# Where the first four weight slots behind a norm are split: all in front of it, or one in front and three among the scaled chunks

## What is computed

```python
def rms_norm(x, g):
    y = x * rsqrt(mean(x * x, -1) + 1e-5)
    return y * g
h = x
p = rms_norm(h, norm_mix) @ w_in                        # "mix"
...
h = h + square(relu(rms_norm(h, norm_mlp) @ w_up)) @ w_down     # "mlp"
x = rms_norm(h, norm_final)                             # "final"
n = rmsnorm(x, g0) * (1 + scale0) + shift0              # "g0", scale and shift from silu(c) @ ada_w
z = gelu(n @ a_w_in) ...                                # its v half is the stage "a_v"
x = x + gate0 * mixed
n = rmsnorm(x, g1) * (1 + scale1) + shift1              # "g1"
x = x + gate1 * conv_ffn(n)                             # "ffn"
```

## Time and profile before

| | us |
|---|---|
| median of three runs | 2870.2 (2868.9 to 2871.1) |
| the profiled execution, its own time | 2871.4 |
| its span in the trace | 2869.5 |
| PE busy | 2745.0 (96%) |
| DVE busy | 2027.0 (71%) |
| ACT busy | 1399.7 (49%) |
| POOL busy | 177.8 (6%) |

### The profile page before, as it was taken

How to read it: one execution, slowest core, us unless ns; L and a number is a source line. 1 busy time by engine, 2 the same in 40 slices (tenths; PEclk the granted TensorE clock), 3 DMA queues, 4 the chain that set the end, 5 groups by cost and what they waited for, 6 DMA issues and landing times.

```text
span 2869.5 us, 48840 instructions
## 1 busy us (share of the span) xinstructions
PE 2745.0 (96%) x17766; PEld 2358.8 (82%) x17766; DVE 2027.0 (71%) x3149; ACT 1399.7 (49%) x2217; POOL 177.8 (6%) x210
## 2 busy tenths in 40 slices
PE   7999988799799999999999999999989999999997
PEld 6878877688588888888886888888868888888886
DVE  5676555577688787888888776668877756665675
ACT  5444443455554444444454455445455545554553
POOL 4600000030100000000020000000100000000002
PEclk9999999899899999999999999999999999999999
DMA  5554200245367778777776874567745555555553
GB/s 192 181 164 163 97 2 2 100 166 188 128 246 281 273 279 292 272 278 279 272 274 222 295 264 164 180 232 276 277 148 184 187 189 181 193 184 188 187 179 137
DMA packets 157857, 573.42 MB, mean 200 GB/s; under 512 B 18000, under 2 KB 18416, under 8 KB 157264
## 3 DMA queue, kind: packets, MB, share of 16 engines
q1 hardware_dynamic: 154368, 562.11, 56.6%
q10 hardware_dynamic: 2208, 7.57, 0.7%
q0 software_dynamic: 1072, 0.89, 0.1%
HBM read 567.64 MB, written 2.10 MB: 199 GB/s over the span
## 4 chain that ended last, share of the span: by engine, by line
PE 83%; DVE 9%; POOL 3%; issue 2%; ACT 2%; DMA 0%; ACTq 0%; DVEq 0%; POOLq 0%
PE ps L2212 44%; PE ps L2213 24%; PE ps L2215 3%; DVE wlo L1896 3%; PE ps L2237 2%; PE ps L2239 2%; PE ps L2238 2%; PE ps L1002 1%; ACT whi L1681 1%; DVE tt L1923 1%; DVE tt L1981 1%; PE ps L1001 1%; PE ps L990 1%; PE ps L1572 0%; POOL tab L285 0%
## 5 line engine op out<-in xcount | busy, mean ns | idle before, releaser
L1896 DVE TENSOR_TENSOR wlo<-raw,whi 128x1024 fp32r<-128x1024 f32 x872 | 1060.9, 1231 | 429.4 <-ACT whi L1681 427.7
L2212 PE MATMUL ps<-xn,whi 128*128 128x512 f32 x3540 | 1259.3, 400 | 11.5 <-issue 5.3
L1681 ACT ACTIVATE whi<-raw 128x1024 fp32r<-128x1024 f32 x872 | 905.0, 1054 | 593.9 <-PE ps L2213 515.0
L2213 PE MATMUL ps<-xn,wlo 128*128 128x256 f32 x3776 | 1052.5, 281 | 0.0
L2212 PE MATMUL ps<-act_in,whi 128*128 128x512 f32 x2444 | 868.5, 400 | 7.7 <-issue 3.4
L2212 PEld LDWEIGHTS ps<-xn,whi 128*128 128x128 f32 x3540 | 667.8, 189 | 177.4 <-issue 11.1
L2213 PE MATMUL ps<-act_in,wlo 128*128 128x256 f32 x2624 | 730.6, 281 | 0.0
L2213 PEld LDWEIGHTS ps<-xn,wlo 128*128 128x128 f32 x3776 | 716.0, 190 | 5.1
L2212 PEld LDWEIGHTS ps<-act_in,whi 128*128 128x128 f32 x2444 | 461.2, 189 | 121.2 <-DVE wlo L1896 5.0
L2213 PEld LDWEIGHTS ps<-act_in,wlo 128*128 128x128 f32 x2624 | 497.6, 190 | 4.0
L1688 ACT ACTIVATE hl<-ps 128x256 f32<-128x256 f32 x416 | 155.3, 375 | 356.9 <-PE ps L2215 356.9
(11 more groups left out here) (329 smaller groups left out, 2226.0 us busy)
## 6 DMA issues: line engine op xcount, KB each, us to landing
raw<-in_stream SPq DMA_DIRECT2D x872, 512.0 KB, 4.2
adaw<-in_ada SPq DMA_DIRECT2D x96, 512.0 KB, 5.9
adaq<-in_ada SPq DMA_DIRECT2D x96, 512.0 KB, 4.8
h<-in_xT SPq DMA_DIRECT2D x4, 512.0 KB, 7.4
memx<-in_memT ACTq DMA_DIRECT2D x1, 2048.0 KB, 9.3
out<-fin SPq DMA_DIRECT2D x4, 512.0 KB, 2.6
lwa<-in_lora ACTq DMA_DIRECT2D x1, 1536.0 KB, 6.9
wst<-in_wsT ACTq DMA_DIRECT2D x1, 1024.0 KB, 8.4
```

What stands on the lines that cost most here:

```text
L1681: act.activation(whi[:, r, :], raw[:, r, :], ACT.Copy).then_inc(hi_done, 1)
L1896: dve.tensor_tensor(wlo[:, r, :], raw[:, r, :], whi[:, r, :].bitcast(F32), ALU.subtract)\
L2212: pe.matmul(ps[:, b, :], whi[:, r, w], x[:, kc, :], start=first, stop=False)
L2213: ins = pe.matmul(ps[:, b, 0:T], wlo[:, r, w], x[:, kc, 0:T], start=False, stop=False)
```

## The change

Behind the norms `mlp`, `g0` and `g1` the split of the next stage's first four slots is taken out of the stage before (`LATE`). Slot 0 is split by ACT in front of the norm and by DVE behind its small steps; slots 1 to 3 are split among the chunks of `prepare`: on DVE after chunks 2, 4 and 6; on ACT slot 1 in front of chunk 0 and slots 2 and 3 in front of chunks 3 and 5. The same at the kernel's beginning, where also: `ones` is set by POOL and not loaded; ACT loads the table of the root ahead of the squares (it holds the square too) and does `silu` after `prepare`; PE does 20 matmuls of `ones` with `ones` (128 x 128) before its first sum and waits for `ident` only before the spread.

```diff
+    LATE = ("q", "o", "mlp", "a_uo")
...
+        pool.memset(ones[:, :], 1.0).then_inc(cols_zero, 1)
...
-        act.dma_start(ones[:, :], A["const"][:, C_ONES, :]).then_inc(const_in, 16)
...
             for j in chunks:
+                if ahead and j in (3, 5):
+                    ahead(0, (j + 1) // 2)
                 act.wait_ge(xp_done, XP[nm] + j + 1)
...
-                     nm == "w_in" or nm in AHEAD.values(), split(L[AHEAD[nm]]) if nm in AHEAD and nm != "q" else None, aside, nm in TAIL_FIRST)
+                     nm == "w_in" or nm in AHEAD.values(), split(L[AHEAD[nm]]) if nm in AHEAD and nm not in LATE else None, aside, nm in TAIL_FIRST)
...
         act.wait_ge(cols_zero, 2)
+        preload(act, ACT.Sqrt)
         for q in range(4):
             act.wait_ge(x_in[q], 16)
             squares(h, tt, 0, range(4 * q, 4 * q + 4))
-        for p in range(RING):
-            split(L["w_in"])(0, p)
+        split(L["w_in"])(0, 0)
+        norm("mix")
+        split(L["w_in"])(0, 1)
+        prepare("mix", ahead=split(L["w_in"]))
         act.wait_ge(par_in, 16)
-        act.wait_ge(cols_zero, 2)
         act.activation(silu_c[:, :], col("c", 0, DC), ACT.Silu).then_inc(silu_done, 1)
-        norm("mix")
-        prepare("mix")
...
+        split(L["mlp"])(0, 0)
         norm("mlp")
-        prepare("mlp")
+        split(L["mlp"])(0, 1)
+        prepare("mlp", ahead=split(L["mlp"]))
...
                 if j:
                     low(j - 1)
+                if ahead and j in (2, 4, 6):
+                    ahead(0, j // 2)
...
-        for p in range(RING):
-            split(L["w_in"])(0, p)
         norm("mix", EPS_1)
-        prepare("mix", h, lambda j: col("norm_mix", j))
+        split(L["w_in"])(0, 0)
+        prepare("mix", h, lambda j: col("norm_mix", j), ahead=split(L["w_in"]))
...
         norm("final", EPS_1)
         norm("g0", EPS_2)
+        split(L["a_v"])(0, 0)
...
-        prepare("g0", h, lambda j: nfg[:, j:j + 1], 0)
+        prepare("g0", h, lambda j: nfg[:, j:j + 1], 0, ahead=split(L["a_v"]))
...
-        pe.wait_ge(const_in, 32)
-        pe.wait_ge(cols_zero, 5)
+        pe.wait_ge(cols_zero, 6)
+        for _ in range(20):
+            pe.matmul(ps[:, stat_bank["mix"] + 2, 0:P], ones[:, :], ones[:, :], start=True, stop=True)
...
+        pe.wait_ge(const_in, 16)
         spread("mix")
```

More of the change, by code:

```diff
@@ L1699, in norm, with prepare @@
             act.activation(y, x, ACT.Sqrt, scale=-2.0).then_inc(rs_done, 1)
-        def prepare(nm, shift=None, chunks=range(DC)):
+        def prepare(nm, shift=None, chunks=range(DC), ahead=None):
             dst, x = act_in if nm == "cross" else xn, sqm if nm == "mem" else tt
             for j in chunks:
+                if ahead and j in (3, 5):
+                    ahead(0, (j + 1) // 2)
                 act.wait_ge(xp_done, XP[nm] + j + 1)
@@ L1816, in _ @@
         rows("g0", ada, 16)
+        split(L["a_v"])(0, 1)
         act.wait_ge(mod_done, 1)
@@ L1819, in _ @@
         act.dma_start(bsb[:, :, :], A["bsb"]).then_inc(mix_in, 16)
-        prepare("g0", 0)
+        prepare("g0", 0, ahead=split(L["a_v"]))
         def a_v(lin, i, g, b):
@@ L1847, in _ @@
         run("a_uo", a_uo)
+        split(L["ffn"])(0, 0)
         norm("g1")
         rows("g1", adb, 8)
-        prepare("g1", 48)
+        split(L["ffn"])(0, 1)
+        prepare("g1", 48, ahead=split(L["ffn"]))
         def ffn(nm, up):
@@ L1961, in scale_of, with prepare @@
             return ps[:, spread_bank[nm], 0:T]
-        def prepare(nm, src, gain, shift=None, chunks=range(DC)):
+        def prepare(nm, src, gain, shift=None, chunks=range(DC), ahead=None):
             dst, x = act_in if nm == "cross" else xn, sqm if nm == "mem" else tt
@@ L2067, in _ @@
         norm("mlp", EPS_1)
-        prepare("mlp", h, lambda j: col("norm_mlp", j))
+        split(L["mlp"])(0, 0)
+        prepare("mlp", h, lambda j: col("norm_mlp", j), ahead=split(L["mlp"]))
         def mlp(lin, i, g, t):
@@ L2137, in _ @@
         norm("g1", EPS_2)
+        split(L["ffn"])(0, 0)
         dve.wait_ge(ada_red, 4)
         modulation(64, 32, 64, "g1")
-        prepare("g1", h, lambda j: mod[:, 96 + DC + j:97 + DC + j], 48)
+        prepare("g1", h, lambda j: mod[:, 96 + DC + j:97 + DC + j], 48, ahead=split(L["ffn"]))
         dve.memset(zc[:, :, 0:1], 0.0).then_inc(pads, 1)
```

## The result

The changed kernel is slightly slower, 0.1 to 0.3%; the interval of the ratio leaves out 1.

What follows compares the result with a forecast made beforehand. PE, busy 96% of the span, was taken as the bound. Terms -4.8 (beginning with tables), +0.1 (`mlp`), +3.4 (`g0`), +0.1 (`g1`) and 3 x 1.5 (clock) gave +3.3 on 2870.2: 2873.5 us, range 2866.5 to 2879.

Steps and rivals of the forecast that it cites:

- sums end: At the beginning, after the warm-up, eight chunks at full clock and eight slow: sums end near 18.7, not 23.84.
- beginning at slot 4: First chunk of `w_in` 8.4 us earlier, but splits and `silu` delay slot 4: ready at 41.5, not 45.02; -3.5 us.
- clock behind it: Low clock after PE's new wait for slot 4: +1.5 us each at the beginning, `mlp` and `ffn`, bounds 0 and 2.5.
- wait for the tables gone: POOL starts the tables earlier, so PE's 1.26 us wait behind ACT's 4.37 us wait for them goes: -1.3 us.
- `mlp` at slot 4: First chunk 3.3 us earlier, slot 4 3.4 later behind it: +0.1 us before the clock.
- `a_v` at slot 4: At `g0` the first chunk stays and three splits lengthen PE's wait: +3.4 us, bounds 2.8 and 4.2.
- Rival E: Faster: the ring does not gate slot 4, head starts stay and no clock falls, about 2856 us; chance 0.05.
- Rival C: At the beginning the warm-up's clock holds through all sums, first chunk at 18.3, total 2870.3 us; chance 0.12.
- rival D: Slower: PE's clock is lost for longer, the warm-up gives nothing, slot 4 at 46.4; 2878.4 us; chance 0.15.
- `silu`: At the beginning ACT's `silu` with its table load, ahead of slot 4's split, delays that split by 1.5 us.
- A: The forecast itself, clock falls charged at the beginning, `mlp` and `ffn`: 2873.5 us, spread 2871 to 2876.5; chance 0.45.
- B: PE's waits grow as forecast but the clock falls at one site or none: about 2869.5 us; chance 0.20.

Runs made afterwards that it cites:

- `a_v` alone: Only the splits of `a_v` moved behind the norm, the beginning, `mlp` and `ffn` as in the kernel before: 2880.8 us, ratio 1.0017 to before.
- two inside: Changed kernel with two splits among the chunks in place of three, `silu` later, root's table earlier, `a_v` as before: 2863.8 us, ratio 0.9966 to before.
- three in front: Changed kernel with three of `a_v`'s splits ahead of the modulation at `g0` and one among the chunks: 2874.2 us, ratio 1.0014 to before.
- without `a_v`: Changed kernel with the norm `g0` and the stage `a_v` put back as before: 2871.7 us, ratio 0.9991 to before.
- again: The kernel before, unedited, profiled a second time: 2872.5 us.
- `mlp` and `ffn` alone: Only the norms `mlp` and `g1` changed, the beginning and `a_v` as in the kernel before: 2874.5 us, ratio 1.0000 to before.
- beginning alone: Only the beginning changed, the three later norms as in the kernel before: 2870.2 us, ratio 0.9983 to before.
- `silu` later: Changed kernel with ACT's `silu` moved from in front of slot 4's split into the groups of `w_in`: 2873.3 us, ratio 1.0003 to before.

## Why the prediction came out as it did

| term | forecast | trace of after |
|---|---|---|
| sums end | 18.7 | 18.07 |
| first chunk of `w_in` scaled | 21.5 | 20.77 |
| PE's wait for slot 4 of `w_in` | 4.9 | 5.44 |
| beginning at slot 4 | -3.5 | -4.2 |
| clock behind it | +1.5 | +2.4 |
| wait for the tables gone | -1.3 | -1.8 |
| `mlp` at slot 4; clock | +0.1; +1.5 | -0.1; 0 |
| `a_v` at slot 4; clock | +3.4; 0 | +3.3; +0.5 |
| `ffn` at slot 4; clock | +0.1; +1.5 | -0.1; +1.5 |
| 260 to 766 us | no term | +3.1 |
| elsewhere, rounding | 0 | +0.6 |
| sum | +3.3 | +5.2 |

**Right: the mechanism, at every place.** A split inside the run over the chunks delays slot 4 by its full length. The three cost 3.4 us in `a_v`, where the norm waits for PE and nothing is given back: +3.3 in after, +3.2 with `a_v` alone, 0 without it. In `mlp` and `ffn` the head start of 3.3 is spent on the same three splits: -0.1 in after and in the experiment of these two alone. Rival E (the ring doesn't gate) is out: PE waits for `wlo` at slot 4 of all four, and two splits in place of three bring 1.1 us at each of `mlp` and `ffn`. (By its own terms E's sum is 2855.2, not 2856.)

**Right: the sums.** Eight chunks fast and eight slow is what the rows show, 3.63 and 6.68 us. Rival C, that the clock holds through the sums, is out, and so is rival D, that the warm-up gives nothing: without it slot 4 is 2.3 us later. The advice of the Trainium skill ("TensorE: Matmul & The Clock Gate", "Why this matters for your kernels"), to keep TensorE busy continuously, is not enough here: the one-column sums keep it busy without a pause over 0.21 us, and neither raise its clock (without the warm-up all 64 run slowly, 13.79 us) nor hold it.

**Right: `silu`.** 1.5 us were charged for a table load and its function; taking them away gave 1.5 between ACT's last chunk and slot 4. By the 2.66 us of the Trainium skill ("ScalarE: Activation LUTs", "What ACT_TABLE_LOAD costs") it would have been 1.4 more; the trace has 1.28 us and the next instruction right behind it.

**Only partly shown: the tables.** ACT's wait for them is gone in after, and 1.8 us with it. But with the beginning as before (`a_v` alone) the same place gained 1.3 us in one trace, where ACT waited 2.58 us in place of 4.37; and with two inside ACT waited 4.20 again and nothing was gained. So part of the 1.8 may be chance.

**Wrong: the clock at each place, though its sum came out.** "I take 1.5" for each fall, at three places: measured are 2.4, 0 and 1.5, and 0.5 more in `a_v`, 4.4 together for the 4.5 forecast. That is luck. The step assumed that a wait of over 2.63 us makes the clock fall. At the same place in `mlp`, 2.98 us did not (after), while 2.52 (three in front), 2.66 and 3.96 did; in `a_v`, 2.63 us did (before) and 2.67 did not (without `a_v`). The wait's length alone does not decide. Behind waits of over 5 us (at `w_in` and `a_v` in after) the low stretch was 6.8 us in place of 3.4, but it was 6.8 also at `ffn` behind 2.63 us (without `a_v`) and 2.86 (three in front). Two of the three falls charged came in after: not all three, as A has it, and not one or none, as B has it.

**Wrong: that the rest stands still.** This is the step that failed: the sum had no term for the stretches that the diff does not touch, it took 2870.2, the median of three runs, for the time of the kernel before, and it called everything within 0.2% "same". The runs show each of the three to be off. In its trace after lost 3.1 us in an untouched stretch. Nine runs of before have a median of 2873.5, 3.3 above the base: that is the whole distance between the time forecast, 2873.5, and the 2876.5 measured, for the medians differ by 3.0 where 3.3 were forecast. And the interval of the ratio, 1.0012 to 1.0029, is half as wide as the 0.2% taken for the resolution to either side: a loss of the size forecast, 3.3 us or 0.11%, is about what it can tell from nothing.

Between 259 and 766 us the shift rises, in each trace, by:

| beginning | kernel: rise, us |
|---|---|
| as before | again -0.6; `a_v` alone +9.9; `mlp` and `ffn` alone -0.1 |
| changed | after +3.1; without `a_v` +6.5; beginning alone +7.8; `silu` later +0.8; three in front +0.7; two inside +0.5 |
| changed, no warm-up | after's +4.1; two inside +1.9 |

No instruction of this stretch differs within the first line from the kernel before, and its instructions are the same in the others but for one early load of the root's table in the two kernels with two inside. The rise goes from -0.6 to +9.9 in one line and from +0.5 to +7.8 in the others. So a rise of 3.1 in one trace is no evidence on the change. That it goes with the clock shows in the executions of the kernel before, 71 beside the experiments, sorted by the mean granted clock over the whole execution:

| mean granted clock | 0.983 | 0.982 | 0.981 | 0.980 | 0.979 | 0.977 |
|---|---|---|---|---|---|---|
| executions | 8 | 15 | 18 | 18 | 6 | 4 |
| mean time, us | 2870.4 | 2871.1 | 2873.0 | 2874.6 | 2877.1 | 2881.3 |

(Two more had 0.978 and 0.975: 2879.5 and 2883.9 us.) The means rise by 11 us as the clock falls from 0.983 to 0.977, three times the effect that the forecast argued about; single executions of this one program reach from 2868.1 to 2884.9.

**What stays open.** By its own places the change costs 5.2 - 3.1 - 0.6 = 1.5 us in the trace; the medians say 3.0 and the ratio 5.7 (3.4 to 8.3). The parts measured alone give -4.9, +4.9 and 0.0 by their ratios, 0 together, and -3.9, +6.8 and +2.6 by their medians, 5.5 together, each with about 3 us either way. The runs are not enough to say whether the remainder is chance, or whether the new beginning makes low clock in the middle somewhat more frequent. That the lines of the table above overlap speaks for chance, and so does the beginning alone, which over twelve runs kept its 3.9 to 4.9 us where its own place gave 4.4; neither shows it. All rises are also taken against one trace of before that was faster than most. The places and the waits are settled, and so is that after is not faster; how much slower it is, 1.5 us or nearer 6, and what the part beyond its own places is, is not.

## What to carry to other kernels

When work is moved from in front of a run into the run, ask when the first thing *behind* it is ready, not only when the run starts: here 9.1 us of earlier start became 4.3 at slot 4, and at three norms nothing or a loss. A split belongs into a wait that the engine has anyway (for the sum, for the spread); with two there and two in the run, with `silu` moved away and `a_v` left as it was, the same idea gained 8 us. Before a difference of a few microseconds is read from two traces, read the same difference from two traces of one kernel, by the starts of the n-th instruction of one kind.

## What the hardware showed that I had not expected

- The clock that 6.5 us of full matmuls had raised fell 4.1 us after they ended, in the midst of one-column matmuls that followed each other without a gap; it stayed low for 13.7 us, through sums and spread and into `w_in`.
- The granted clock reads 1.00 until its first recorded change: without the warm-up it does so from 10 to 20 us, while the sums run at the slow pace of the earlier trace rows (48 passes in 10 us). At the start of a trace the durations tell the clock, the column does not. So mean clocks are compared above only among executions of one kernel.
- At slot 4, waits of PE of 1.22, 1.38, 1.60 and 2.37 us cost no clock, 2.25, 2.52, 2.63, 2.66, 2.82, 3.02, 3.86 and longer ones did, 2.67 and 2.98 did not. The low stretch there was recorded as 3.4 or 6.8 us; it cost 1.3 to 1.7 us (3.4), and 2.4 (at `w_in` in after) to 2.9 (at `ffn` without `a_v`) where it was 6.8.
- The same program is granted a mean clock from 0.977 to 0.983 on one chip and from 0.975 to 0.983 on another, and the largest piece of it that the traces show lies between 260 and 780 us, where PE works with pauses: 0.94 and 0.91, 8 us of PE's time apart.
